# Feed-forward's second product as seven block products with sums of blocks, quarter by quarter

## What is computed

```python
h = rmsnorm(x, pre_ffn_g[l]) @ w_ffn_up[l]      # 512 x 1024 @ 1024 x 4096
f = jnp.square(jax.nn.relu(h)) @ w_ffn_down[l]  # 512 x 4096 @ 4096 x 1024
x = x + rmsnorm(f, post_ffn_g[l])
```

## Time and profile before

| what | value |
|---|---|
| time, median of 3 runs | 2912.66 us (2908.76 to 2913.89) |
| time of the profiled execution | 2906.96 us |
| its span from first to last instruction | 2905.0 us |
| mean granted TensorE clock | 0.989 of full |
| TensorE busy | 2804.1 us, 97% |
| VectorE, ScalarE, GpSimd busy | 1602.1, 1168.1 and 724.0 us |

### The profile page before, as it was taken

The page is one execution under the profiler, slowest core; times in us unless marked ns, Lnnn a source line. Parts: engine busy times, 40 slices in busy tenths (PEclk is TensorE's granted clock), DMA queues, the critical chain, the costliest instruction groups (busy, mean ns, idle before and its releaser), DMA issues.

```text
span 2905.0 us, 34935 instructions
## 1 busy us (share of the span) xinstructions
PE 2804.1 (97%) x13382; PEld 2321.1 (80%) x13382; DVE 1602.1 (55%) x2156; ACT 1168.1 (40%) x1855; POOL 724.0 (25%) x604
## 2 busy tenths in 40 slices
PE   8898999999999989999999999999999999999998
PEld 6676888888877768878888788888887779888887
DVE  5787446334267874464543786555434468555532
ACT  5576234222245663242122555333222348432222
POOL 2464113314014641134041240122200014122210
PEclk9999999999999999999999999999999989999999
DMA  4011322322221102223232212223232210122232
GB/s 140 30 44 33 99 94 82 101 94 97 100 80 37 37 30 95 94 86 104 94 101 95 78 57 70 95 96 101 95 108 95 87 44 1 59 102 94 95 102 100
DMA packets 73974, 235.70 MB, mean 81 GB/s; under 512 B 9136, under 2 KB 17600, under 8 KB 73824
## 3 DMA queue, kind: packets, MB, share of 16 engines
q1 hardware_dynamic: 72624, 230.26, 23.8%
q0 software_dynamic: 928, 3.27, 0.4%
q10 hardware_dynamic: 272, 0.06, 0.0%
HBM read 228.31 MB, written 2.10 MB: 79 GB/s over the span
## 4 chain that ended last, share of the span: by engine, by line
PE 86%; DVE 8%; ACT 3%; issue 1%; POOL 1%; DMA 1%; SPq 0%; POOLq 0%; DVEq 0%; ACTq 0%
PE bank L2116 27%; PE bank L2118 26%; PE bank L2117 26%; PE bank L2547 2%; PE bank L2364 1%; DVE STAT L1772 1%; DMA RAWW<-weights 1%; DVE X L1671 1%; DVE WL L1642 1%; DVE UL L1659 1%; DVE FF L1666 1%; ACT WH L1282 1%; PE bank L2451 1%; DVE PHL L1647 0%; PE bank L2307 0%
## 5 line engine op out<-in xcount | busy, mean ns | idle before, releaser
L1642 DVE TENSOR_TENSOR WL<-RAWW,WH 128x1024 fp32r<-128x1024 f32 (+2 forms) x421 | 569.8, 1357 | 740.4 <-ACT WH L1282 740.2
L2116 PE MATMUL bank<-UH,WH 128*128 128x512 f32 (+2 forms) x1968 | 768.5, 390 | 33.6 <-DVE UL L1659 11.7
L2117 PE MATMUL bank<-UL,WH 128*128 128x512 f32 (+2 forms) x1968 | 759.5, 386 | 0.0
L2118 PE MATMUL bank<-UH,WL 128*128 128x512 f32 (+2 forms) x1968 | 759.4, 386 | 0.0
L1282 ACT ACTIVATE WH<-RAWW 128x1024 fp32r<-128x1024 f32 (+2 forms) x424 | 431.3, 1027 | 393.8 <-DMA RAWW<-weights 393.1
L2116 PEld LDWEIGHTS bank<-UH,WH 128*128 128x128 f32 (+1 forms) x1968 | 371.4, 189 | 119.5 <-issue 22.3
L2117 PEld LDWEIGHTS bank<-UL,WH 128*128 128x128 f32 (+1 forms) x1968 | 371.7, 189 | 75.1 <-issue 2.4
L2118 PEld LDWEIGHTS bank<-UH,WL 128*128 128x128 f32 (+1 forms) x1968 | 371.6, 189 | 75.1
L2116 PE MATMUL bank<-HH,WH 128*128 128x512 f32 (+1 forms) x576 | 210.8, 366 | 0.0
L2118 PE MATMUL bank<-HH,WL 128*128 128x512 f32 (+1 forms) x576 | 210.5, 365 | 0.0
L2117 PE MATMUL bank<-HL,WH 128*128 128x512 f32 (+1 forms) x576 | 210.5, 365 | 0.0
(11 more groups left out here) (363 smaller groups left out, 4703.2 us busy)
## 6 DMA issues: line engine op xcount, KB each, us to landing
RAWW<-weights SPq DMA_DIRECT2D x424, 512.0 KB, 3.5
X<-x SPq DMA_DIRECT2D x8, 256.0 KB, 5.5
FF<-tables POOLq DMA_DIRECT2D x2, 1024.0 KB, 7.5
U<-S5U SPq DMA_DIRECT2D x32, 64.0 KB, 2.0
out<-FF SPq DMA_DIRECT2D x16, 128.0 KB, 1.8
GEL<-U SPq DMA_DIRECT2D x64, 16.0 KB, 1.8
S5B<-s_b POOLq DMA_DIRECT2D x1, 512.0 KB, 4.6
S5C<-s_c POOLq DMA_DIRECT2D x1, 512.0 KB, 3.9
```

Source lines behind the costliest of these rows:

```text
L1642: dve.tensor_tensor(slot_words(WL, c % SLOTS, size), slot_words(RAWW, c % SLOTS, size), f32(slot_words(WH, c % SLOTS, size)), ALU.subtract ...
L2116: nc.tensor.matmul(out_, w[0], x_[0], start=start, stop=False, **how)
L2117: nc.tensor.matmul(out_, w[0], x_[1], start=False, stop=False, **how)
L2118: return nc.tensor.matmul(out_, w[1], x_[0], start=False, stop=stop, **how)
```

## The change

**Seven products for eight.** The second product now runs in four quarters of 8 hidden tiles. In the first three quarters, two output tiles are made at once, a *duo*: the weights are a 2x2 grid of blocks (two output tiles by two groups of four hidden tiles), the hidden values another one (the two groups by two halves of the tokens). Instead of eight block products it does seven, on sums and differences of blocks. Each is 4 x 3 = 12 matmuls of 256 columns. There are 4 duos in a quarter, 12 in a layer, 24 in all. In the order in which TensorE does them, with the bank half they go to (banks x and y):

| | to | weights by hidden | waits for |
|---|---|---|---|
| P1 | y front | s1 by t1 | s1's low part, t1's low part |
| P2 | x front | a11 by front | the cut of the duo's first chunk |
| P3 | y front | s4 by low_tail | s4's low part, the add FIFTH |
| P4 | x front | s2 by t2 | s2's low part, FIRST_ALONE |
| P5 | y back | s3 by t3 | the cut of the second chunk, THIRD_IN |
| P6 | x back | a12 by tail | SIXTH_IN |
| P7 | y back | a22 by t4 | SEVENTH |

**Sums of weights.** s1 = a21 + a22, s2 = s1 - a11 (VectorE), s4 = a12 - s2, s3 = a11 - a21 in place (GpSimd). They are 128 x 512 floats each. s1, s2 and s4 also need a high part (ScalarE) and a low part (VectorE). They are made for the next duo inside the current one (`duo_prepare`).

**Sums of hidden values.** t1 to t4, 256 columns for each of four pairs of hidden tiles (`sum_one`, `sum_rest`), four subtractions or additions on VectorE, high parts on ScalarE, low parts on VectorE, while the hidden tiles are made. The tiles come in the order 0, 4, 1, 5, 2, 6, 3, 7.

**Adds out of the banks.** Seven for a duo, all on VectorE, 256 columns wide but for SIXTH_IN, which adds one bank half to three halves of `FF` in one instruction of 768 (in the first quarter in three of 256). VectorE's queue in a duo is: SECOND_AGAIN and FOURTH_IN of the duo before with s4's low part between them, FIFTH, s2's low part, FIRST_ALONE, THIRD_IN, the cut of the second chunk, SIXTH_IN, then for the next duo s1, s2 and s1's low part, then SEVENTH, then the cut of the next duo's first chunk, which waits until GpSimd has made both of its sums.

**Ahead of the first duo.** The first up job of the next quarter is run between the last up job and the duos (`lead_in`). The fourth quarter stays as before, with 8 jobs of one chunk; the last pair is now one chunk deep, and all of the 256-column work before the norm is 96 matmuls in a layer.

**Moved.** `state_params` goes to the gates and branches of layer 0 (tile 2), `pole_powers` in seven parts to the second quarter's `evac_up` of layer 1, `state_input` to the fourth quarter's `evac_up`, `turn_grid` in four parts behind it. A few semaphores are merged.

The diff, cut to what the prediction speaks of:

```diff
+def raised_tiles(plan, q, norm):
+    job = dict(cols=P, kt=[DT], rhs="u")
+    whole = q == QUARTERS - 1
+    order = range(DT) if whole else UP_ORDER
+    done = {}
+    def evac(i, mm, held=None):
+        done[i] = plan.add("evac_up", "up", i=i, m=order[i], q=q, j=mm.j, bank=mm.bank, done=mm.c, held=held,
+                           front=not whole and order[i] < DT // 2,
+                           summed=min(q * DUOS + i // 2, LAYER_DUOS))
+        if i:
+            sums_of(i - 1)
+    def sums_of(i):
+        if whole:
+            return
+        if i % 2 == 0:
+            plan.add("sum_one", "t1", k=order[i], up=done[i].up)
+        else:
+            plan.add("sum_rest", "tr", k=order[i - 1], up=done[i].up)
+    def lead_in():
+        mm = plan.add("mm", "c j", first=False, ring=2, **job)
+        mm.bank = mm.j % 2
+        plan.led = mm
+        prepare(plan, 0, q)
+    first = 0
+    if q:
+        evac(0, plan.led, plan.total["c"] - 1)
+        first = 1
+    linear(plan, [job] * (DT - first), dict(norm=norm, evac=lambda x, mm: evac(x + first, mm), then=None if whole else lead_in))
+    if not whole:
+        plan.add("duo_low", which="s1", **plan.next_duo)
+        sums_of(DT - 1)
+        plan.add("duo_low", which="a1", **plan.next_duo)
+        plan.last_up = done[DT - 1]
+def prepare(plan, p, q):
+    c = plan.total["c"]
+    assert plan.cut == c
+    plan.cut = c + 2
+    plan.next_duo = dict(c=c, duo=plan.total.get("duo", 0), m=2 * p, q=q)
+    plan.add("duo_prepare", **plan.next_duo)
+def lowered_quarter(plan, q):
+    before = None
+    for p in range(DUOS):
+        info = plan.next_duo
+        st = plan.add("duo", "c:2 duo", m=2 * p, q=q, last_up=plan.last_up.up if p == 0 else None, last_j=plan.last_up.j)
++        if before:
+            plan.add("duo_add", which=SECOND_AGAIN, **before)
+        plan.add("duo_low", which="s4", **info)
+        if before:
+            plan.add("duo_add", which=FOURTH_IN, **before)
+        plan.add("duo_add", which=FIFTH, **info)
+        plan.add("duo_low", which="s2", **info)
+        plan.add("duo_add", which=FIRST_ALONE, **info)
+        plan.add("duo_add", which=THIRD_IN, **info)
+        plan.add("duo_low", which="a2", **info)
+        plan.add("duo_add", which=SIXTH_IN, **info)
+        if p < DUOS - 1:
+            prepare(plan, p + 1, q)
+            plan.add("duo_low", which="s1", **plan.next_duo)
+        else:
+            plan.cut_to(plan.total["c"])
+        plan.add("duo_add", which=SEVENTH, **info)
+        if p < DUOS - 1:
+            plan.add("duo_low", which="a1", **plan.next_duo)
+        before = info
+    plan.add("duo_add", which=SECOND_AGAIN, **before)
+    plan.add("duo_add", which=FOURTH_IN, **before)
...
-    for half in range(2):
-        linear(plan, [dict(tile, rhs="u")] * HALF,
-               dict(norm=None if half else norm,
-                    evac=lambda x, mm: plan.add("evac_up", "up", m=x, j=mm.j, bank=mm.bank, done=mm.c)))
-        pair = linear(plan, [dict(cols=P, kt=[DT, DT], rhs="hidden")] * DT,
-                      dict(ahead="post" if half else None, evac=into_ff(half == 1, POST_FFN if half else None),
-                           add=half == 1, group=POST_FFN))
+    for q in range(QUARTERS - 1):
+        raised_tiles(plan, q, norm if q == 0 else None)
+        lowered_quarter(plan, q)
+    raised_tiles(plan, QUARTERS - 1, None)
+    pair = linear(plan, [dict(tile, rhs="hidden")] * DT,
+                  dict(ahead="post", evac=into_ff(True, POST_FFN), add=True, group=POST_FFN))
...
+                    if l * LAYER_DUOS + st.summed:
+                        pool.wait_ge(hid_sum.sem, nth(hid_sum, 4, l, st.summed - 1, 3))
...
+                elif st.kind == "duo_prepare":
+                    a11, a12 = (block_of(RAWW, st.c, k) for k in range(2))
+                    a21 = block_of(RAWW, st.c + 1, 0)
+                    s2, s4 = (weight_sum(k)[2] for k in ("s2", "s4"))
+                    pool.wait_ge(duo_sum.sem, nth(duo_sum, 4, l, st.duo, 1))
+                    pool.tensor_tensor(s4, a12, s2, ALU.subtract).then_inc(duo_sum.sem, 1)
+                    pool.tensor_tensor(a21, a11, a21, ALU.subtract).then_inc(duo_sum.sem, 1)
...
+                elif kind == "sum_one":
+                    act.wait_ge(hid_sum.sem, nth(hid_sum, 4, l, st.t1, 0))
+                    act.activation(TH[:, 0, st.k, :], TF[:, 0, st.k, :], ACT.Copy).then_inc(hid_sum_h.sem, 1)
+                elif kind == "sum_rest":
+                    act.wait_ge(hid_sum.sem, nth(hid_sum, 4, l, st.tr, 3))
+                    act.activation(TH[:, 1:4, st.k, :], TF[:, 1:4, st.k, :], ACT.Copy).then_inc(hid_sum_h.sem, 1)
+                elif kind == "duo_prepare":
+                    for i, which in enumerate(("s1", "s2", "s4")):
+                        high, low, made = weight_sum(which)
+                        act.wait_ge(duo_sum.sem, nth(duo_sum, 4, l, st.duo, i))
+                        act.activation(high, made, ACT.Copy).then_inc(duo_h.sem, 1)
+                        if i == 0:
+                            cut(l, st.c, SLOT)
+                    act.wait_ge(duo_sum.sem, nth(duo_sum, 4, l, st.duo, 3))
+                    cut(l, st.c + 1, SLOT)
...
+                elif kind == "sum_rest":
+                    f, g = TMP[:, 0, :], TMP[:, 1, :]
+                    t2, t3, t4 = (TF[:, i, st.k, :] for i in (1, 2, 3))
+                    dve.wait_ge(hid_f.sem, hid_f.after(l, st.up))
+                    dve.tensor_tensor(t3, g[:, BACK], f[:, BACK], ALU.subtract).then_inc(hid_sum.sem, 1)
+                    dve.wait_ge(hid_sum.sem, nth(hid_sum, 4, l, st.tr, 1))
+                    dve.tensor_tensor(t2, t3, f[:, FRONT], ALU.add).then_inc(hid_sum.sem, 1)
+                    dve.wait_ge(hid_sum.sem, nth(hid_sum, 4, l, st.tr, 2))
+                    dve.tensor_tensor(t4, g[:, FRONT], t2, ALU.subtract).then_inc(hid_sum.sem, 1)
+                    dve.wait_ge(hid_sum_h.sem, nth(hid_sum_h, 2, l, st.tr, 1))
+                    rest(TL[:, 1:4, st.k, :], TF[:, 1:4, st.k, :], TH[:, 1:4, st.k, :]).then_inc(hid_sum_l.sem, 1)
+                elif kind == "duo_low" and st.which in ("a1", "a2"):
+                    if st.which == "a1":
+                        dve.wait_ge(duo_sum.sem, nth(duo_sum, 4, l, st.duo, 3))
+                    cut(l, st.c + (st.which == "a2"), SLOT)
+                elif kind == "duo_low":
+                    high, low, made = weight_sum(st.which)
+                    dve.wait_ge(duo_h.sem, nth(duo_h, 3, l, st.duo, ("s1", "s2", "s4").index(st.which)))
+                    if st.which == "s1":
+                        dve.wait_ge(duo_sum.sem, nth(duo_sum, 4, l, st.duo, 1))
+                    rest(low, made, high).then_inc(duo_l.sem, 1)
+                elif kind == "duo_prepare":
+                    a11 = block_of(RAWW, st.c, 0)
+                    a21, a22 = (block_of(RAWW, st.c + 1, k) for k in range(2))
+                    s1, s2 = (weight_sum(k)[2] for k in ("s1", "s2"))
+                    older = l * LAYER_DUOS + st.duo
+                    for c in (st.c, st.c + 1):
+                        dve.wait_ge(raw_in[c % SLOTS], l * (CHUNKS_L // SLOTS * 16) + 16 * (c // SLOTS + 1))
+                    if older:
+                        dve.wait_ge(duo_pe.sem, nth(duo_pe, 5, l, st.duo - 1, 0))
+                    dve.tensor_tensor(s1, a21, a22, ALU.add).then_inc(duo_sum.sem, 1)
+                    dve.wait_ge(duo_sum.sem, nth(duo_sum, 4, l, st.duo, 0))
+                    if older:
+                        dve.wait_ge(duo_pe.sem, nth(duo_pe, 5, l, st.duo - 1, 3))
+                    dve.tensor_tensor(s2, s1, a11, ALU.subtract).then_inc(duo_sum.sem, 1)
...
+                elif kind == "duo_add":
+                    x, y = (BANK[k] for k in DUO_BANKS[st.duo % 2])
+                    first, part, a, b = st.q == 0, st.which, FF[:, st.m, :], FF[:, st.m + 1, :]
+                    if part in (SECOND_AGAIN, FOURTH_IN):
+                        dve.wait_ge(used.sem, used.after(l, st.c + (part == FOURTH_IN)))
+                    else:
+                        dve.wait_ge(duo_pe.sem, nth(duo_pe, 5, l, st.duo, part))
...
+                    elif part == SIXTH_IN:
+                        dve.wait_ge(duo_added.sem, nth(duo_added, 7, l, st.duo, THIRD_IN))
+                        if first:
+                            dve.tensor_tensor(a[:, BACK], x[:, FRONT], a[:, BACK], ALU.add)
+                            dve.tensor_copy(b[:, FRONT], x[:, FRONT])
+                            ins = dve.tensor_tensor(b[:, BACK], x[:, FRONT], b[:, BACK], ALU.add)
+                        else:
+                            three = FF[:, st.m:st.m + 2, :].rearrange("p k n -> p (k n)")[:, SEQ // 2:].rearrange("p (k n) -> p k n", k=3)
+                            ins = dve.tensor_tensor(three, x[:, FRONT].unsqueeze(1).to_broadcast([P, 3, SEQ // 2]), three, ALU.add)
+                    elif part == SEVENTH:
```

(29 more changed lines are left out.)

268 lines of the change are left out of this document (184 added, 84 removed).

## The result

| | before | after |
|---|---|---|
| median of the runs | 2910.71 us (2906.39 to 2913.89) | 2975.29 us (2972.64 to 2984.96) |
| profiled execution | 2906.96 us | 2984.96 us |
| its span, mean granted clock | 2905.0 us, 0.989 | 2983.1 us, 0.981 |
| TensorE / VectorE / ScalarE / GpSimd busy | 2804.1 / 1602.1 / 1168.1 / 724.0 us | 2817.6 / 1844.2 / 1232.8 / 795.1 us |

The changed kernel takes 1.0229 times the time of the one before, 95% interval 1.0201 to 1.0257. Forecast were 2955 us, range 2924 to 2990: the sign is right, the time is inside the range of 2924 to 2990 but outside 2940 to 2968, which the forecast itself, without its rivals, had been given, and the median is 20 us above the forecast.

What follows compares the result with a forecast made beforehand. TensorE was taken to bound the kernel: 2906.96 - 20.5 (matmuls) + 60.9 (quarters' stalls) + 0.8 (SIXTH_IN) + 4 (`state_params`) = 2952.2 us; with half the median's 5.7 offset 2955 us, range 2924 to 2990.

Steps and rivals of the forecast that it cites:

- the forecast itself, without its rivals: Whole kernel: the forecast's own range of 2940 to 2968 us, given 47%.
- The matmuls: Second product: 256-column matmuls 0.120 us apart, 10.08 us in a duo; 10.2 us less a layer, 20.5 in all.
- The 28.6 us: Second product: the matmul saving estimated by the Trainium skill's gap formula alone, beside the 20.5 us from the rows.
- That VectorE's chain would hold TensorE: Duos and entries: TensorE idle ahead of P7 for SEVENTH, ahead of P5 and P2 for a cut, twice at each entry.
- Rivals 1, 2 and 5: TensorE stays the bound, 2889 us, 10%; lock free in duos, lower entry, 2930, 17%; near break-even, 2907 to 2915, 6%.
- The steady duo: Duos behind a quarter's first: period 11.65 us, with s1's low part taking its turn before s4.
- rival 3: Duos: GpSimd takes its turns first, 0.43 to 1.73 us more for 18 duos, 2963 to 2986 us; 13%.
- The entry: First duo of each quarter: P1 2.0 us late, P4 4.9 late in all, the same for six quarters.
- A fall of the clock: Quarter entries: granted clock falls after TensorE's stalls, six times 2 us, 2967 us; 7%.
- `state_input` "hidden, at worst 2 us late": Layer 1's last quarter: 3.8 us more VectorE work in every second tile, hidden by slack, at worst 2 us late.
- `state_params` in the gates: Gates: ScalarE's wait for GpSimd and table loads make TensorE late once, 4 us, bounds 0 and 6.
- `pole_powers`, which I had at nothing: Beside full up and down tiles: listed among the things that cost nothing.

Runs made afterwards that it cites:

- c6: Changed kernel with two lead jobs, all weight sums on VectorE, SEVENTH and second chunk's cut earlier, `state_params` moved back, `state_input` in eight parts: 2917.45 us.
- c10: c9 with VectorE's entry queue reordered: weight sums, s1's low part and first cut ahead of the last tile's hidden sums, their low parts behind FIFTH: 2908.05 us.
- x1: Changed kernel with sums of weights whole only for a layer's first duo, elsewhere on one element of each partition: 2941.48 us.
- e5: Changed kernel with GpSimd's s4 started only after s1's low part, outside a quarter's first duo: 2973.84 us.
- e46: Changed kernel with `state_params` back beside the second product and `state_input` on even instead of odd up tiles: 2975.74 us.
- e8: Changed kernel with two lead jobs instead of one ahead of the duos, last tile's sums ahead of the sums of weights: 2950.01 us.
- c9: c6 with the low parts of the hidden sums one step later in VectorE's queue and `state_input` in twelve parts: 2919.48 us.
- e1: Changed kernel with SEVENTH ahead of s1's low part of the next duo in VectorE's queue: 2974.18 us.
- e2: Changed kernel with the entry's first cut ahead of the last tile's hidden sums, these behind FIFTH of the first duo: 2972.27 us.
- x2: Changed kernel with sums of hidden values cut to one column in a layer's second and third quarter: 2964.89 us.

## Why the prediction was right, and where its sizes were off

**The matmuls: right.** 256-column matmuls are 0.12 apart inside a block product, and a duo with no wait takes 10.15 to 10.17 us (c6, c10) where 10.08 were forecast. The 10.2 us a layer are there, less 0.08 for each of 12 duos. (The 28.6 us that the prediction sets beside its 20.5 come to 28.8 by the formula given there; nothing rests on it.)

**That VectorE's chain would hold TensorE: right.** TensorE is idle ahead of P7 behind SEVENTH, ahead of P5 behind a cut, and twice at each entry, as listed. Rivals 1, 2 and 5 are out as this kernel stands. x1 shows what it hangs on: take the sums' work away and all steady waits but P5's go.

**The steady duo: 11.65 forecast, 12.12 to 12.24 measured.** The step that failed is the choice of who takes the free turn: I let s1's low part go ahead of s4, "since VectorE's own dependency (0.03) is shorter than a release of GpSimd". It was 0.10 here against 0.08, GpSimd was first by 0.02, and the wait ahead of P7, 1.47 to 1.6 (once 1.77), stands in 17 of the 18 duos that prepare another; in the eighteenth VectorE was first by 0.04, and it was 0.34. e5, which forces the forecast's order, brings it to the same 0.36. That is the lower end of rival 3 (0.43 more), which I had at 13%; its bound of 12.1 was met to 0.02. The sum of a quarter hides it in part: I gave each quarter's last duo 1.18 of stalls and it has 0.47 (10.55 for 10.08).

**The entry: right for four quarters, wrong for two.** 4.7 us for P1 and P2 forecast, 4.85 measured. A second or third quarter stalls for 11.6 us in all against 10.15 forecast (layer 1's third for 14.2, with slow matmuls behind P1). But I took one entry for all six. The first quarter of a layer follows the norm, and VectorE comes to the last up tile's bank 3 us later: 16.6 and 17.8 us of stalls, slow matmuls included. That the norm is what puts it behind is read from this place; no run took the norm away, and c10 shows that the order of the queue at the entry, too, held P1 up (from 3.3 us late to 1.2 and 0.4). The rows for it were there (the up tiles of before show VectorE's place in them), and I hadn't followed them from the norm on. The six quarters sum to 83.5 us, 82.8 without the 0.1 too much for each P1, against 61.7: this is the miss. A fall of the clock was a rival of its own (4, six times 2 us); it came, but at the long waits above all, on top of the forecast and not in its place.

**`state_input` "hidden, at worst 2 us late": wrong.** 4.7 us. I had averaged 3.8 us over two tiles; a single part is 5.7 to 6.3 us in one piece with a cut behind it. e46 and e8 moved the wait and c9, with pieces of 2.5 to 3.1 us, took most of it away.

**`state_params` in the gates: 4 forecast, 1.8 measured**, and moving it gave all of that back; the stage's other 1.2 us are slow matmuls at its start that come without it too.

**Sum.** -20.5 + 82.8 + 4.7 + 1.8 = 68.8, of the 78.1 of the profile. In the 82.8 are 0.6 by which P1 of layer 1's second quarter is later than that of layer 0's; `pole_powers`, which I had at nothing, hangs on the up tiles there. Of the other 9.3, 2.5 lie in the feed-forwards outside all of this (1.7 in layer 0, where the first up tiles ran at a granted clock of 0.72 from 478 to 484 us, for 1.00 before), 1.2 at the start of the gates, 1.6 elsewhere ahead of the first feed-forward, -0.8 between the two and 4.8 behind the second.

The profiled execution's 9.7 us over its median go with the lowest granted clock of the four (0.981 for 0.983 to 0.985). In which stages the other three kept it isn't known: only one was profiled.

## What to carry to other kernels

Fewer products buy only what the engine that makes their operands has to spare; add up that engine's queue over the period, and its longest dependent chain, before counting matmuls. Two engines that share one chain through a lock are no relief: give the whole chain to the faster one, and put its queue in the order in which the consumer asks. Cost an entry for each kind of predecessor separately, and a moved preparation by its longest piece against the slack of one tile; done that way, the change came from 2.3% slower to level, and not beyond, for all of its 20 us fewer in matmuls.

## What the runs showed of the hardware

**The clock after a wait.** P1 of a first quarter came, in the profiles of this study, after an idle TensorE of different lengths. After 4.0 to 5.9 us (18 times) its matmuls started 0.23 us apart, but once 0.17 on the mean: that is the lower of the two levels, 1.2 for 2.4 GHz. After 3.1 to 3.3 us (e8, c6, c9) the mean was 0.23 three times, 0.19 and 0.13 once each. After 2.1 to 2.8 us in later quarters (20 times, in the kernel after, e1, e2, e5 and e46) it was 0.13 or 0.14 in 13, 0.15 to 0.17 in three and 0.19 to 0.23 in four: 0.21 in layer 1's third quarter of the changed kernel, for one, and 0.13 in e46 at the same place behind the same wait. In x2 the first duos of the first quarters took 3.1 and 3.4 us more than their matmuls and their own waits together: that is what a wait of 5 us ahead of P1 costs beyond itself. The Trainium skill (TensorE: Matmul & The Clock Gate, "HAM oscillation") says that idle gaps put the array back to half rate; the longest gaps here agree, and of the shorter ones some were followed by it and some not.

**A lead of 0.02 us decided 1.1.** When s2 released GpSimd and VectorE together, GpSimd was first by 0.02 us 17 times, and VectorE's 0.69 us instruction took 1.80 to 1.82; once VectorE was first by 0.04, and took 0.69. In the rows of before I had seen only cases where one of them was clearly first.
